# One pipeline over the 64 level steps of all heads in the recurrent scan

## The reference, cut to what matters

```
o_inter = einsum('bthk,bhkv->bthv', qc * exp(bcs), S)
diff = bcs[:, :, None] - bcs[:, None]
dec = exp(where(mask, diff, -inf))
att = einsum('bthk,btshk,bshk->bhts', qc, dec, kc)
o_intra = einsum('bhts,bshv->bthv', att, vc)
S_new = S * exp(last)[..., None] + einsum('bshk,bshv->bhkv', kc * exp(last[:, None] - bcs), vc)
```

## Time and profile before

| | |
|---|---|
| median of 3 runs | 3088.2 us (3087.59 to 3092.51) |
| the profiled execution | 3088.64 us, of which the span is 3086.8 us |
| PE busy | 2676.4 us, 87% of the span |
| DVE, ACT, POOL busy | 1495.7, 745.3, 802.0 us |
| mean granted TensorE clock | 0.909 of full speed |

### The profile page before, as it was taken

The page is one execution under the profiler, slowest core; times in us unless marked ns, Lnnn a source line. Parts: engine busy times, 40 slices in busy tenths (PEclk is TensorE's granted clock), DMA queues, the critical chain, the costliest instruction groups (busy, mean ns, idle before and its releaser), DMA issues.

```text
span 3086.8 us, 30672 instructions
## 1 busy us (share of the span) xinstructions
PE 2676.4 (87%) x11926; PEld 1965.5 (64%) x11926; DVE 1495.7 (48%) x2416; ACT 745.3 (24%) x1253; POOL 802.0 (26%) x501
## 2 busy tenths in 40 slices
PE   1689889997986678899998877778999989989997
PEld 1679864445975667854447876667544579975444
DVE  7546543334546775633334567886223325650012
ACT  0123130002442233210013233332100134221101
POOL 1346300002432235200004556661000146610000
PEclk9889889998898889899998987777999999979999
DMA  6443639891320114558872420104698533436881
GB/s 218 164 126 94 193 118 352 325 351 64 113 96 28 42 44 120 191 206 333 323 267 75 150 84 19 33 26 154 245 343 328 214 96 110 137 123 241 298 299 54
DMA packets 291856, 524.44 MB, mean 170 GB/s; under 512 B 9473, under 2 KB 141057, under 8 KB 291329
## 3 DMA queue, kind: packets, MB, share of 16 engines
q1 hardware_dynamic: 288256, 519.33, 47.8%
q10 hardware_dynamic: 3456, 3.15, 0.3%
HBM read 517.73 MB, written 4.72 MB: 169 GB/s over the span
## 4 chain that ended last, share of the span: by engine, by line
PE 73%; DVE 16%; issue 3%; ACT 3%; DMA 3%; POOL 2%; ACTq 0%; SPq 0%; DVEq 0%
PE ps L1631 22%; PE ps L1646 11%; PE ps L1443 6%; PE ps L1444 6%; PE ps L1445 6%; PE ps L1477 3%; DVE macc L1710 3%; PE ps L650 2%; PE ps L1466 2%; PE ps L1493 2%; PE ps L1467 2%; PE ps L1468 2%; DVE h L1740 1%; POOL wlo L1376 1%; PE ps L1571 1%
## 5 line engine op out<-in xcount | busy, mean ns | idle before, releaser
L1376 POOL TENSOR_TENSOR wlo<-ring,whi 128x1024 fp32r<-128x1024 f32 x202 | 527.7, 2627 | 1546.2 <-ACT whi L1248 1546.2
L1631 PE MATMUL ps<-ring,xg 128*128 128x512 f32 x1536 | 704.9, 603 | 0.0
L1631 PEld LDWEIGHTS ps<-ring,xg 128*128 128x128 f32 x1536 | 289.3, 194 | 327.6 <-issue 327.3
L1710 DVE SCALAR_TENSOR_TENSOR macc<-ring,cond_s,macc 128x1024 f32<-128x1024 f32 x336 | 450.8, 1403 | 0.0
L1921 DVE SCALAR_TENSOR_TENSOR hid<-ps,cws,sg 128x256 f32<-128x256 f32 x96 | 46.4, 484 | 671.3 <-ACT sg L1341 671.3
L1646 PE MATMUL ps<-ring,hidt 128*128 128x512 f32 x768 | 354.2, 605 | 2.3 <-ACT hidt L1315 2.3
L1443 PE MATMUL ps<-hh,whi 128*128 128x384 f32 x832 | 304.1, 366 | 27.0 <-POOL wlo L1376 17.1
L1248 ACT ACTIVATE whi<-ring 128x1024 fp32r<-128x1024 f32 x202 | 206.9, 1054 | 379.5 <-DMA ring<-gmlp_w_out 115.2
L1444 PE MATMUL ps<-hl,whi 128*128 128x384 f32 x832 | 290.1, 349 | 0.0
L1445 PE MATMUL ps<-hh,wlo 128*128 128x384 f32 x832 | 289.9, 348 | 0.0
L1646 PEld LDWEIGHTS ps<-ring,hidt 128*128 128x128 f32 x768 | 148.8, 194 | 190.2 <-issue 190.2
(11 more groups left out here) (325 smaller groups left out, 4233.1 us busy)
## 6 DMA issues: line engine op xcount, KB each, us to landing
ring<-moe_w_gu SPq DMA_DIRECT2D x192, 1024.0 KB, 7.6
ring<-w_mod SPq DMA_DIRECT2D x96, 1024.0 KB, 7.5
ring<-moe_w_down SPq DMA_DIRECT2D x96, 1024.0 KB, 5.0
ring<-gmlp_w_in SPq DMA_DIRECT2D x32, 1024.0 KB, 5.7
ring<-ssd_w_in SPq DMA_DIRECT2D x21, 1024.0 KB, 5.2
ring<-hgrn_w_in SPq DMA_DIRECT2D x20, 1024.0 KB, 5.2
ring<-gmlp_w_out SPq DMA_DIRECT2D x16, 1024.0 KB, 5.8
ring<-ssd_w_out SPq DMA_DIRECT2D x8, 1024.0 KB, 5.9
```

The lines of the kernel that those rows point to most:

```text
L1376: pool.tensor_tensor(split_sub(wlo, s0), raw_sub(s0), split_sub(whi, s0).bitcast(F32), ALU.subtract).then_inc(S["lo_ready"], 1)
L1631: ins = pe.matmul(ps[:, s % 2, :], xg[:, w, k, :], whole(what, s, 4)[:, k % 4, :], start=(k == 0), stop=(k == KD - 1))
L1710: ins = dve.scalar_tensor_tensor(out=macc[:, v, :], in0=w[:, k, :], scalar=by, in1=macc[:, v, :], op0=ALU.mult, op1=ALU.add)
```

## The change

Three things are changed, all in the four loops over heads.

First, the border difference of both halves becomes one operation, and so does the multiplication by the keys. The two directions of `hf` (and `hk`) lie one behind the other, so a pattern with a negative or shifted step between its two rows reaches the left halves in the one and the right halves in the other: 384 columns in place of two times 192. The tensors get 128 more columns so that the pattern stays inside.

Second, the loops over heads and levels become one over `NS = 64` steps. The differences are made two steps ahead and the keys completed one step ahead, across the border of a head too.

Third, the keys, transposes and states of head h+1 are spread over the levels of head h, and the output of head h-1 follows the first product of head h.

The core of the diff:

```diff
-            for h in range(HH):
-                for j in range(4):
-                    n, (t, d) = 4 * h + j, STATES[j]
-                    dve.wait_ge(S["kh_exp"], n + 1)
-                    dve.tensor_tensor(hkh[:, n % 2, :], hkh[:, n % 2, :], hk[:, d, h, toks(t)], ALU.mult).then_inc(S["kh_ready"], 1)
...
-                    dve.tensor_tensor(U[:, :, 0, :], rf, F[:, :, 0, :], ALU.subtract)
-                    dve.tensor_tensor(U[:, :, 1, :], rg, G[:, :, 1, :], ALU.subtract).then_inc(S["u_sub"], 1)
...
+        def two_rows(a, start, stride):
+            return a[:, start:start + 2 * stride].rearrange("p (two y) -> p two y", two=2)
+        def blocks(a, x, j):
+            return a[:, :, x:x + T].rearrange("p two (b x) -> p b two x", x=2 << j)[:, :, :, 0:1 << j]
+        def paired(a, h, j):
+            return blocks(two_rows(a, 0, span + (1 << j)), h * T, j)
+        def border(h, j, rev=False):
+            a = two_rows(hf_flat, 0, span + 1)
+            a = a[:, ::-1, :] if rev else a
+            a = a[:, :, h * T + (1 << j) - 1:(h + 1) * T:2 << j].rearrange("p two b -> p b two")
+            return a.unsqueeze(3).to_broadcast([P, T // (2 << j), 2, 1 << j])
...
+            def produce(g):
+                h, j = divmod(g, HL)
+                if j:
+                    if g >= 3:
+                        dve.wait_ge(S["lv_done"], g - 2)
+                    out = uw_slot(g)[:, 0, :].rearrange("p (b two x) -> p b two x", two=2, x=1 << (j - 1))
+                    dve.tensor_tensor(out, border(h, j - 1), paired(hf_flat, h, j - 1), ALU.subtract).then_inc(S["u_sub"], 1)
...
+            for g in range(NS):
+                h, j = divmod(g, HL)
+                if g + 2 < NS:
+                    produce(g + 2)
+                if g + 1 < NS:
+                    complete(g + 1)
+                if j in (1, 2):
+                    carry(h, j + 1)
+                if h + 1 < HH:
+                    if 3 <= j <= 6:
+                        key_turned(h + 1, j - 3)
+                    if 1 <= j <= 4:
+                        key(h + 1, j - 1)
+                pick(g)
```

POOL and ACT, in the same loop over levels (on ACT the exponential of level index j comes first, then what follows here):

```diff
+            for n in range(LEVELS * HH):
+                h, j = divmod(n, LEVELS)
+                if n + 1 < LEVELS * HH:
+                    decay(n + 1)
+                pool.wait_ge(S["u_exp"], n + 1)
+                W = uw_slot(HL * h + j + 1)[:, 1, :]
+                pool.tensor_tensor(W, W, hq[:, h, :], ALU.mult).then_inc(S["wq_ready"], 1)
...
+                    if j < 4 and more:
+                        key_decay(h + 1, j)
+                    if j == 2:
+                        if h:
+                            head_over(h - 1)
+                        act.activation(hqe[:, :, :], hf[:, :, h, LC:T], ACT.Exp).then_inc(S["qe_exp"], 1)
```

More of the change, by code:

```diff
@@ L880, in head_over, with key_decay, state_decay @@
                 act.activation(hk[:, 1, h, :], bank(2), ACT.Square).then_inc(S["o_read"], 1)
-            for h in range(HH):
[L883 to L895, removed]
+            def key_decay(h, i):
+                n, (t, d) = 4 * h + i, STATES[i]
+                act.wait_ge(S["scan_ready"], 8 + h + 1)
+                if n >= 2:
+                    act.wait_ge(S["khT_done"], n - 1)
+                last = t * P + (P - 1 if d == 0 else 0)
+                act.activation(hkh[:, n % 2, :], hf[:, d, h, toks(t)], ACT.Exp, scale=-1.0,
+                               bias=hf[:, d, h, last:last + 1]).then_inc(S["kh_exp"], 1)
+            def state_decay(h):
                 for j in (2, 3):
@@ L901, in act_hgrn, with state_out @@
                     act.activation(hed[:, d:d + 1], hf[:, d, h, last:last + 1], ACT.Exp).then_inc(S["edec_ready"], 1)
[L902 to L908, removed]
+            def state_out(h, j):
+                act.wait_ge(S["hst_done"], 4 * h + j + 1)
+                if h:
+                    act.wait_ge(hst_out[j], 16 * h)
+                act.activation(hsto[j][:, :], ps[:, 6 + j, 0:P], ACT.Copy).then_inc(S["stout_read"], 1)
+                act.wait_ge(S["stout_read"], 2 * SG_ + 2 * h + j + 1)
+                act.dma_start(O["n_hgrn"][:, j, h, :], hsto[j][:, :]).then_inc(hst_out[j], 16)
+            for i in range(4):
+                key_decay(0, i)
+            state_out(0, 0)
+            state_out(0, 1)
+            for h in range(HH):
+                more = h + 1 < HH
                 for j in range(LEVELS):
@@ L1059, in pe_hgrn, with output @@
+            def output(h):
+                pe.wait_ge(S["lv_read"], HL * (h + 1))
                 pe.wait_ge(S["qe_ready"], h + 1)
@@ L1062, in pe_hgrn @@
                     pe.wait_ge(S["o_read"], h)
+                hc = slice(h * P, (h + 1) * P)
                 for t in range(NT):
@@ L1069, in pe_hgrn @@
                 ins.then_inc(S["o_done"], 1)
+            for i in range(4):
+                turn(0, i)
+                if i:
+                    state(0, i - 1)
+            state(0, 3)
+            for n in range(NS):
+                h, j = divmod(n, HL)
+                pe.wait_ge(S["uw_ready"], n + 1)
+                if j:
+                    pe.wait_ge(S["wq_ready"], LEVELS * h + j)
+                if n >= 2:
+                    pe.wait_ge(S["lv_read"], n - 1)
+                for t in range(NT):
+                    rhs = uw_slot(n)[:, 1, toks(t)] if j else hq[:, h, toks(t)]
+                    ins = pe.matmul(ps[:, n % 2, toks(t)], uw_slot(n)[:, 0, toks(t)], rhs, start=True, stop=True)
+                ins.then_inc(S["lv_done"], 1)
+                if j == 0 and h:
+                    state(h, 3)
+                    output(h - 1)
+                gate_step(h, j)
+                if j == 4 and h:
+                    square_sums(h - 1)
+                if h + 1 < HH:
+                    if 2 <= j <= 5:
+                        turn(h + 1, j - 2)
+                    if 4 <= j <= 5:
+                        state(h + 1, j - 4)
+                    if j == 7:
+                        state(h + 1, 2)
+            output(HH - 1)
             square_sums(HH - 1)
@@ new lines, in dve_hgrn @@
+            for i in range(4):
+                key(0, i)
+                key_turned(0, i)
+            produce(1)
+            complete(0)
+            for g in range(NS):
+                h, j = divmod(g, HL)
+                if g + 2 < NS:
[4 more added lines that the diff above has]
+                    carry(h, j + 1)
+                if h + 1 < HH:
+                    if 3 <= j <= 6:
[3 more added lines that the diff above has]
+                pick(g)
```

198 lines of the change are left out of this document (90 added, 108 removed).

## The result

The changed kernel takes 3056.8 us (median of 4 runs, 3053.9 to 3062.3) against 3089.3 for the kernel before beside it (3087.6 to 3092.5): ratio 0.9892, 95% interval 0.9875 to 0.9910. That is 32.5 us less, where 25.4 were forecast, and near the lower end of the range of 3056 to 3072. The profiled execution took 3059.1 us with a span of 3057.3.

The account below looks back on a forecast made before the run. DVE and POOL taking turns bind the levels: 23.0 us of turns a head, 24.1 with the clock; eight heads, plus drain, less edge savings, make 194.2 against 219.6, 25.4 less. Forecast 3063 us, range 3056 to 3072.

Parts of the forecast that it names:

- The bound: In the scan's levels, DVE operations with two SBUF inputs and POOL operations exclude each other; their turns make 2.72 us.
- Its own signs: Scan trace: key sums 23 to 25 us apart, levels 2.6 to 2.8, clock 0.85 or more, merged DVE 0.55, POOL 0.99.
- one sign of being wrong: ACT's L920 waiting behind L890 for a transpose, listed among the signs that would show the prediction wrong.
- Merging by itself brings next to nothing.: Seven levels of a head: a merged level takes 2.60 to 2.80 us, 0.12 less to 0.08 more than 2.72.
- POOL ... two such, 1.74 at best: Each level's two merged POOL operations of 384 columns, priced like L972 (0.99 alone, 0.12 less behind a release); 1.94 back to back.
- Spreading keys and states: Between heads: takes 7.1 us and the last levels' drain off the path, adds their DVE and POOL work to the levels.
- The clock's term: TensorE in the scan: a quarter of levels at 1.2 GHz, 27.5 against 23.0 us a head, giving 24.1.
- ACT's queue: ACT at level 4's exponential, behind a key waiting for a transpose: just in time at 2.4 GHz, 1.5 us late at 1.2.
- It costs nothing in the sum: Verdict on ACT's queue: no cost per head, up to 2 us if the estimate is off.
- that rival: ACT's queue late at every head by 1.5 to 2.5 us, or turns not closing up: 26 us a head, 3078; chance 18%.
- the output ahead of the pick of step 0: DVE waits about 4 us behind level 7's product, filled by POOL's low weights and next turns; nothing at 2.4 GHz.

Follow-up runs that it names:

- merge_only: The kernel before, in its old order, with only the three merged operations of 384 columns; 3076.5 us, ratio 0.9957, scan 221.5 us.
- filler: The changed kernel with three more 128x128 products in each level on TensorE, their result not read; 3058.8 us, ratio 0.9880, scan 196.9 us.
- out_later: The changed kernel with ScalarE's output copy, square and `hqe` exponential moved from level index 2 to 4, dependent work later too; 3061.7 us, ratio 0.9898.
- both moves: The changed kernel with out_later's edit and, at each head's last level, GpSimd's query product before the next head's first difference; 3048.5 us, ratio 0.9862.
- again: The changed kernel, unedited, run once more; 3059.6 us, ratio 0.9905, scan 200.1 us.

## Why the prediction was right, and where its terms were off

**The bound.** Right, and shown: VectorE and GpSimd taking turns made up the level before (2.72), make it up in merge_only (2.41), and work cut on either shortens the scan and the other's operations. After the change one of the two is in such an operation for 130.1 of 141 us.

**Its own signs.** Two came: key sums 23.4 us apart and VectorE's merged operations at 0.53. Three did not: levels of 2.6 to 2.8 in all eight, a granted clock of 0.85 or more (it was 0.78), GpSimd's merged difference at 0.99 (it was 0.82). And one sign of being wrong came: L920 behind L890, which waits for a transpose. So the number was right with part of the mechanism off, and near the edge of its range.

**"Merging by itself brings next to nothing."** Wrong. It brings 10 to 12 us. The columns cost what was said on VectorE and in the product; the term that failed is "POOL ... two such, 1.74 at best", which priced the merged difference like the product, 0.87 behind a release. It is 0.71. With it seven levels are 16.9 us and a head's turns 16.9 + 4.3 = 21.2, not 22.5 to 23.9.

**Spreading keys and states.** It was to bring all of the 25.4 us, and brought 20.5 to 22.9. That both terms were off, one way each, helped the number.

**The clock's term.** The share of the lower clock was to halve, to a quarter of the levels; at a mean of 0.78 it is (1 - 0.78) / 0.5 = 44%. But the price was 9 us (8 x 1.1) and filler shows some 4. Two errors against each other: the share too small, the cost of a level at 1.2 GHz too high. That they offset is luck.

**ACT's queue.** "It costs nothing in the sum" failed: in heads 1 to 6 the exponential of level 4 is late, as the rival said, by 0.9 to 2.3 us of GpSimd's time in the two traces, though a head did not come to the 26 us of that rival. I counted from the end of GpSimd's product for level 2, but TensorE starts that level only when VectorE's keys are done, a turn of GpSimd later (same kernel, third head, other rows left out):

```profile
1888.79 1.01 POOL L1014 TENSOR_TENSOR uw<-uw,hq 128x384 f32<-128x384 f32 x1
...
1889.83 1.14 POOL L1005 TENSOR_TENSOR uw<-hf 128x384 f32<-128x384 f32 x1
...
1890.13 1.26 DVE L1215 TENSOR_TENSOR uw<-uw,hk 128x384 f32<-128x384 f32 x1
...
1891.44 0.94 PE L1115 MATMUL ps<-uw 128*128 128x128 f32 x6 [1.17 <-DVE uw L1215]
```

The product ends at 1889.80 and TensorE starts at 1891.44, 1.64 us later. The part behind the transpose was right: 2.4 us by the estimate, 1895.52 - 1893.02 = 2.5 in the rows. out_later gave nothing that can be told, since it did not remove GpSimd's wait for exponentials.

**Not in the sum at all**: GpSimd's wait for a buffer at each head's end, up to 2.5 us. The level-0 step takes one of the three buffers without any work of GpSimd in it, so that engine is a buffer short there.

**Balance for a head.** 24.1 were forecast, 23.0 of turns and 1.1 for the clock; 23.4 was measured. By the column "neither" 8% of it, 1.8 us, is time without turns, so the turns take 21.6: 1.4 less than forecast, with 0.7 more beside them. The 1.8 us hold the clock and all waits together; they overlap, so their worths must not be added. With the clock at 1.00 (filler) 1.3 of 22.8 us are left, with both moves 0.7 of 22.4. What is still open is the 0.4 us by which the turns are longer than the 21.2 added up from single rows; the output ahead of the pick of step 0, for which VectorE waits up to 2.3 us a time in the trace of again, is one wait that was not tried.

## What to carry to other kernels

Where two engines exclude each other, add up their turns from the ends of the instructions, not from their durations or busy shares; the sum of one period must come out to the period before it is used for a forecast, and the periods must be alike before one is multiplied. Price a merged operation with a repeated operand from a row of that kind, or keep both ends. When a loop is pipelined across a border, look on each in-order engine for the first operation that waits at the border while the one behind it is ready: turning the two round took 3.6 us off this scan, with a granted clock that rose from 0.78 to 0.89 beside it. And when an edit moves the clock as well, hold the clock up in both versions before the gain is put down to the edit.

## What the runs showed of the hardware that was not expected

- GpSimd's tensor-tensor operation of 384 columns takes 0.82 us with an operand that repeats values and 0.99 to 1.00 with two full ones; with 192 columns and a repeated operand 0.50.
- Stretches of the same code ahead of the scan end anywhere from 1826 to 1839 us in these traces, and the code behind it takes 1018 to 1027 us. A change worth 3 us is seen in the trace of its own stretch, and not in the time of the whole.
